# Last feed-forward sub-layer of a two-layer diffusion trunk: outputs by token rows, gate multiplied into the weights, three weight places; and another order in the opening

## The reference

```python
def rms_norm(x, g):
    y = xf * lax.rsqrt(jnp.mean(xf * xf, axis=-1, keepdims=True) + NORM_EPS)
    return y * g
def swiglu(h, w_in, w_out):
    g, u = jnp.split(h @ w_in, 2, axis=-1)
    return (jax.nn.silu(g) * u) @ w_out
def ffn_sublayer(x, g, shift, scale, gate, w_in, w_out):
    return x + FFN_RES * gate * swiglu(modulate(rms_norm(x, g), shift, scale), w_in, w_out)
...
        x = ffn_sublayer(x, g_norm[i, 2], mx[6], mx[7], mx[8], ffn_w_in[i, 1], ffn_w_out[i, 1])
    return rms_norm(x, g_final)
```

## Time and profile before

| | us |
|---|---|
| median of 3 runs (lowest, highest) | 1735.09 (1732.62, 1735.58) |
| the profiled execution | 1734.88 |
| its span, first to last instruction | 1733.1 |
| PE busy in the span | 1663.2 (96%) |
| DVE busy | 1131.4 (65%) |
| ACT busy | 610.4 (35%) |
| Silu of the first hidden tile of the last sub-layer | 1535.14 |
| last residual addition starts | 1721.27 |

### The profile page before, as it was taken

How to read it: one execution, slowest core, us unless ns; L and a number is a source line. 1 busy time by engine, 2 the same in 40 slices (tenths; PEclk the granted TensorE clock), 3 DMA queues, 4 the chain that set the end, 5 groups by cost and what they waited for, 6 DMA issues and landing times.

```text
span 1733.1 us, 24411 instructions
## 1 busy us (share of the span) xinstructions
PE 1663.2 (96%) x9083; PEld 1427.1 (82%) x9083; DVE 1131.4 (65%) x1934; ACT 610.4 (35%) x825; POOL 138.9 (8%) x82
## 2 busy tenths in 40 slices
PE   5999999999999899999999999999999879989996
PEld 3788888889777798888888988888888867889996
DVE  5778778778575778777877843743335865555555
ACT  3322221234666532212222432122123445353434
POOL 0000000001885100000000000000000222000000
PEclk9999999999999999999999999999999989989999
DMA  7655555541211135555555234422223211145553
GB/s 282 258 207 191 194 191 191 193 152 74 96 50 49 56 121 217 189 194 194 188 195 199 77 119 145 146 97 97 97 97 116 79 64 58 50 143 178 187 172 121
DMA packets 46005, 248.02 MB, mean 143 GB/s; under 512 B 5232, under 2 KB 6384, under 8 KB 25456
## 3 DMA queue, kind: packets, MB, share of 16 engines
q1 hardware_dynamic: 45936, 247.08, 39.7%
HBM read 246.01 MB, written 1.05 MB: 143 GB/s over the span
## 4 chain that ended last, share of the span: by engine, by line
PE 88%; DVE 8%; ACT 2%; issue 1%; DMA 1%; ACTq 0%; POOL 0%; SPq 0%; DVEq 0%
PE ps L1616 15%; PE ps L1618 15%; PE ps L1625 15%; PE ps L1442 10%; PE ps L1443 10%; PE ps L1444 10%; PE ps L1468 3%; PE ps L1754 3%; DVE w_lo L1094 1%; PE ps L1713 1%; PE ps L1652 1%; PE ps L1855 1%; PE ps L1785 1%; PE ps L1671 1%; DVE work L997 1%
## 5 line engine op out<-in xcount | busy, mean ns | idle before, releaser
L1616 PE MATMUL ps<-a_hi,w_hi 128*128 128x512 f32 (+1 forms) x1280 | 451.9, 363 | 3.1 <-ACT w_hi L631 3.1
L1618 PE MATMUL ps<-a_lo,w_hi 128*128 128x512 f32 (+1 forms) x1280 | 451.7, 363 | 0.0
L1094 DVE TENSOR_TENSOR w_lo<-raw,w_hi 128x2048 fp32r<-128x2048 f32 x144 | 329.3, 2289 | 86.7 <-ACT w_hi L631 49.1
L1442 PE MATMUL ps<-h_hi,w_lo 128*128 128x512 f32 (+1 forms) x824 | 285.6, 347 | 4.3 <-DVE w_lo L1094 2.8
L1443 PE MATMUL ps<-h_lo,w_hi 128*128 128x512 f32 (+1 forms) x824 | 283.6, 344 | 0.0
L1444 PE MATMUL ps<-h_hi,w_hi 128*128 128x512 f32 (+1 forms) x824 | 283.5, 344 | 0.0
L1616 PEld LDWEIGHTS ps<-a_hi,w_hi 128*128 128x128 f32 x1280 | 241.7, 189 | 41.4 <-issue 2.5
L1618 PEld LDWEIGHTS ps<-a_lo,w_hi 128*128 128x128 f32 x1280 | 241.9, 189 | 37.2
L1625 PE MATMUL ps<-a_hi,w_lo 128*128 128x512 f32 (+1 forms) x1280 | 269.1, 363 | 0.0
L1625 PEld LDWEIGHTS ps<-a_hi,w_lo 128*128 128x128 f32 x1280 | 220.1, 189 | 37.3
L625 ACT ACTIVATE work<-ps 128x512 f32<-128x512 f32 (+1 forms) x88 | 48.0, 545 | 487.2 <-PE ps L1625 466.6
(11 more groups left out here) (252 smaller groups left out, 1875.9 us busy)
## 6 DMA issues: line engine op xcount, KB each, us to landing
raw<-wstream SPq DMA_DIRECT2D x159, 1024.0 KB, 4.9
mring<-wmod SPq DMA_DIRECT2D x144, 512.0 KB, 3.5
xT<-tokens SPq DMA_DIRECT2D x4, 512.0 KB, 5.3
cb<-cond SPq DMA_DIRECT2D x1, 1024.0 KB, 6.5
out<-spare SPq DMA_DIRECT2D x8, 128.0 KB, 2.0
cst<-consts SPq DMA_DIRECT2D x1, 449.0 KB, 7.1
vec<-vecs SPq DMA_DIRECT2D x1, 174.0 KB, 7.0
ccol<-cond_cols SPq DMA_DIRECT2D x1, 8.0 KB, 1.6
```

The source lines that it names most:

```text
L1094: dve.tensor_tensor(w_lo[:, slot], raw[:, slot], w_hi[:, slot].bitcast(F32), ALU.subtract).then_inc(lo_ready, 1)
L1442: pe.matmul(dst, lhs_lo, rhs_hi, start=start, stop=False, skip_group_check=True)
L1616: pe.matmul(bank, hi, a_hi[:, k, 0:nt], start=k == 0, stop=False, skip_group_check=True)
L1618: pe.matmul(bank, hi, a_lo[:, k, 0:nt], start=False, stop=False, skip_group_check=True)
```

## The change

- **Last sub-layer, products.** The low part of the normalised latent tiles is written into columns 256 to 511 of `a_hi`, beside the high part. An input slab is now 16 matmuls of 512 columns (high weights by high and low activations at once, `last_in`) and 16 of 256 columns (low weights). The bank's two halves have to be added: DVE does this by a `tensor_reduce` over a pair for the gate and one for the up bank (`last_hidden`), and Silu and the product read SBUF.
- **Outputs by token rows.** The outputs are no longer grouped: hidden tiles go in 11 pairs, each with two input slabs and one output slab, in which the stationary operand is the hidden tile (128 tokens) and the moving one the slab (512 output features). Four banks (two token blocks by two feature halves) are kept over the whole sub-layer (`row_product`). They start from the residual, turned by 16 float32 products with the identity (`residual_rows`), 12 of them between the column sums and the spread of the norm, 4 behind the head.
- **The gate** is spread over partitions during the latent attention (8 float32 matmuls of 128 columns on PE, 2 copies on ACT) and multiplied into each raw output slab by DVE (`last_gated`) before its high part is made.
- **Three slab places**: `raw` 0, `raw` 1 and `spare`; the third place's parts lie in `h_hi` and `h_lo`.
- **End.** The squares are summed along rows by ACT (`accum_out`), one inverse root per token block, four stores; no partition sums and no spread.
- **Opening.** Eight buffers for squares, four additions of pairs, the column sums accumulate on PE; 12 matmuls on constants before them; other order of `first_products`; the low parts of slabs 0 and 1 and the high part of slab 1 one tile later; an inverse root of more than two columns takes two instructions a step for four.

The diff, cut to its core:

```diff
+        gate_row = gate_rows[:, 0:D]
+        gain_row, result = mring[:, 0], mring[:, 1:3]
+        raws = (raw[:, 0], raw[:, 1], spare[:])
+        high_slabs = (w_hi[:, 0], w_hi[:, 1], h_hi[:, 4:8].rearrange("p a n -> p (a n)"))
+        low_slabs = (w_lo[:, 0], w_lo[:, 1], h_lo[:, 4:8].rearrange("p a n -> p (a n)"))
...
+            sp.wait_ge(lo_ready, W_FFN3 + 1)
+            last_slab(2)
+            sp.dma_start(gain_row, gain.partition_broadcast(P).rearrange("p a n -> p (a n)")).then_inc(in_gain, 16)
+            with sp.Fori(0, (LAST_SLABS - 3) // 6) as i:
+                for j in range(6):
+                    sp.wait_ge(lo_ready, i * 6 + (W_FFN3 + j + 1))
+                    last_slab(3 + j, i * 6)
...
+                    if i in (2, 5):
+                        n = i // 3
+                        act.wait_ge(gate_spread, n + 1)
+                        act.activation(gate_row[:, n * 512:(n + 1) * 512], ps[2][:], ACT.Copy).then_inc(gate_copy, 1)
...
+            def last_high(r, i=None):
+                k0 = (lambda x: x) if i is None else (lambda x: x + i * 6)
+                if r >= 3:
+                    act.wait_ge(slab_done, k0(W_FFN3 + r - 2))
+                if r % 3 == 1 or r == LAST_SLABS - 1:
+                    n = r // 3 if r % 3 == 1 else LAST_PAIRS
+                    act.wait_ge(slab_gated, n if i is None else i * 2 + n)
+                else:
+                    n = last_loaded(r)
+                    act.wait_ge(raw_loaded[last_place(r)], n if i is None else i * 32 + n)
+                act.activation(high_slabs[last_place(r)], raws[last_place(r)], ACT.Copy).then_inc(hi_ready, 1)
+            def last_hidden(f, i=None):
+                k0 = (lambda x: x) if i is None else (lambda x: x + i * 4)
+                act.wait_ge(gate_sum, k0(f + 1))
+                act.activation(sil[:, f % 2, HIGH_PART], sil[:, f % 2, LOW_PART], ACT.Silu).then_inc(sil_ready, 1)
+                act.wait_ge(pair_free, k0(f0 + f + 3))
+                act.activation(h_hi[:, f % 4, HIGH_PART], prod[:, f % 2, HIGH_PART], ACT.Copy).then_inc(hhi_ready, 1)
+            def last_step(f, r, i=None):
+                for j in range(2):
+                    last_hidden(f + j, i)
+                    if r + j + 3 < LAST_SLABS:
+                        last_high(r + j + 3, i)
+                if r + 5 < LAST_SLABS:
+                    last_high(r + 5, i)
+            last_high(2)
...
+                    if n > 2:
+                        link(dve.tensor_tensor(rt[:, c], y[:, c], y[:, c], ALU.mult))
+                        last = dve.tensor_tensor(rt[:, c], rt[:, c], hv[:, c], ALU.mult)
...
-            first_squares("ffn0", TOK)
-            for k in range(2, DT):
-                add_square("ffn0", k, sq[:, k % 2], ss[:, 0])
+            for k in range(0, DT, 2):
+                dve.wait_ge(sq_ready, k + 2)
+                dve.tensor_tensor(first_sq(k), first_sq(k), first_sq(k + 1), ALU.add).then_inc(ss_sum, 2)
...
-                if k < 2:
-                    split_lo(k, k)
+                if 1 <= k < 3:
+                    split_lo(k - 1, k - 1)
...
+            def last_low(r, i=None):
+                dve.wait_ge(hi_ready, W_FFN3 + r + 1 if i is None else i * 6 + (W_FFN3 + r + 1))
+                at = last_place(r)
+                dve.tensor_tensor(low_slabs[at], raws[at], high_slabs[at].bitcast(F32), ALU.subtract).then_inc(lo_ready, 1)
...
+                pair = raws[at].rearrange("p (a n) -> p a n", a=2)
+                dve.tensor_tensor(pair, pair, gate_row.unsqueeze(1).to_broadcast([P, 2, D]), ALU.mult) \
+                   .then_inc(slab_gated, 1)
...
+                for dst, bank, done in ((sil, 2 * slot, gate_sum), (prod, 2 * slot + 1, up_sum)):
+                    dve.tensor_reduce(dst[:, slot, LOW_PART], ps[bank][:].rearrange("p (a n) -> p n a", a=2), AX.X,
+                                      ALU.add).then_inc(done, 1)
+                dve.wait_ge(up_sum, k0(f + 1))
+                dve.wait_ge(sil_ready, k0(f0 + f + 1))
+                dve.tensor_tensor(prod[:, slot, HIGH_PART], sil[:, slot, HIGH_PART], prod[:, slot, LOW_PART],
+                                  ALU.mult).then_inc(pair_free, 1)
+                dve.wait_ge(hhi_ready, k0(f0 + f + 1))
+                dve.tensor_tensor(h_lo[:, f % 4, HIGH_PART], prod[:, slot, HIGH_PART],
+                                  h_hi[:, f % 4, HIGH_PART].bitcast(F32), ALU.subtract).then_inc(hid_ready, 1)
+            def last_step(f, r, i=None):
+                last_hidden(f, r, i)
+                if r + 3 == LAST_SLABS - 1:
+                    last_gated(r + 3, i)
+                last_low(r + 3, i)
+                last_hidden(f + 1, r + 1, i)
+                if r + 5 < LAST_SLABS:
+                    last_low(r + 4, i)
+                    last_gated(r + 5, i)
+                    last_low(r + 5, i)
+            last_low(2)
+            last_hidden(0, 0)
+            last_low(3)
+            last_hidden(1, 1)
+            last_gated(4)
+            last_low(4)
+            with dve.Fori(0, LAST_TURNS) as i:
+                for _, f, r in LAST_STEPS:
+                    last_step(f, r, i)
+            for _, f, r in END_STEPS:
+                last_step(f, r)
+            dve.wait_ge(in_gain, 16)
+            for b in range(2):
+                dve.wait_ge(row_squares, 2 * b + 1)
+                dve.tensor_tensor(result[:, b, 0:512], row_bank(b, 0)[:], gain_row[:, 0:512],
+                                  ALU.mult).then_inc(row_gained, 1)
+                dve.wait_ge(row_squares, 2 * b + 2)
+                link(dve.tensor_tensor(rt[:, 2 + b:3 + b], squares[:, 2 * b:2 * b + 1],
+                                       squares[:, 2 * b + 1:2 * b + 2], ALU.add))
+                root(rt[:, 2 + b:3 + b], b, 1.0 / D, NORM_EPS)
+                dve.wait_ge(rstd_ready, CALL["final"] + b + 1)
+                dve.scalar_tensor_tensor(out=result[:, b, 512:D], in0=row_bank(b, 1)[:], scalar=ry[:, b:b + 1],
+                                         in1=gain_row[:, 512:D], op0=ALU.mult, op1=ALU.mult).then_inc(y_ready[1], 1)
...
+                    if i in (1, 4):
+                        n = i // 3
+                        if n:
+                            pe.wait_ge(gate_copy, n)
+                        for k in range(4):
+                            m = 4 * n + k
+                            last = pe.matmul(ps[2][:, k * P:(k + 1) * P], gate[:, 5, 0, m:m + 1].to_broadcast([P, P]), ident,
+                                             start=True, stop=True)
+                        last.then_inc(gate_spread, 1)
...
+            for n in range(WARM):
+                pe.matmul(ps[7][:, 0:P], ones[:], ones[:], start=True, stop=True)
+            for k in range(0, DT, 2):
+                pe.wait_ge(ss_sum, k + 2)
+                for c in range(TOK // P):
+                    last = pe.matmul(ps[NORM_BANK][:, c:c + 1], first_sq(k)[:, c * P:(c + 1) * P], ones[:, 0:1],
+                                     start=k == 0 and c == 0, stop=k == DT - 2, skip_group_check=True)
+            last.then_inc(colsum, 1)
...
+                    first_products(1, m - 2, (0, 1))
                 turn_chunk(m)
-            first_products(0, DT - 2)
-            first_products(1, DT - 3)
-            first_products(0, DT - 1)
-            first_products(1, DT - 2)
-            first_products(1, DT - 1)
+                first_products(0, m - 1, (0, 1) if m == 1 else (0, 1, 2))
+                if m == 2:
+                    first_products(0, 0, (2,))
+            first_products(1, DT - 2, (0, 1))
+            for k in range(2):
+                first_products(1, k, (2,))
+            first_products(0, DT - 1, (0, 1, 2), True)
+            first_products(1, DT - 1, (0, 1))
+            for k in range(2, DT):
+                first_products(1, k, (2,), k == DT - 1)
...
+            def residual_rows(b, h):
+                for k in range(4):
+                    pe.matmul(row_bank(b, h)[:, k * P:(k + 1) * P], xT[:, 4 * h + k, b * P:(b + 1) * P], ident,
+                              start=k == 0, stop=False, skip_group_check=True)
+            def last_in(f, r, i=None):
+                slab = W_FFN3 + r + 1
+                at = last_place(r)
+                pe.wait_ge(hi_ready, slab if i is None else i * 6 + slab)
+                pe.wait_ge(pair_free, f0 + f + 1 if i is None else i * 4 + (f0 + f + 1))
+                for t in range(2):
+                    for k in range(DT):
+                        pe.matmul(ps[2 * (f % 2) + t][:], high_slabs[at][:, t * HALF + k * P:t * HALF + (k + 1) * P], a_hi[:, k],
+                                  start=k == 0, stop=False, skip_group_check=True)
+                pe.wait_ge(lo_ready, slab if i is None else i * 6 + slab)
+                for t in range(2):
+                    for k in range(DT):
+                        last = pe.matmul(ps[2 * (f % 2) + t][:, HIGH_PART],
```

(28 more changed lines are left out.)

193 lines of the change are left out of this document (130 added, 63 removed).

## The result

| | us |
|---|---|
| median before, 6 runs (lowest, highest) | 1735.34 (1732.62, 1736.18) |
| median after, 6 runs (lowest, highest) | 1741.95 (1740.75, 1745.46) |
| ratio after to before, 95% interval | 1.0043 (1.0030 to 1.0056) |
| the profiled execution after, and its span | 1745.46, 1743.7 |

The change makes the kernel 6.6 us slower by the medians (their quotient is 1.0038, inside the interval).

The account below looks back on a forecast made before the run. PE bounds the kernel before; after the change DVE and ACT in series bound the last sub-layer. Terms 18.4 + 2.0 - 5.4 + 1.5 - 6.0 = +10.5 on 1734.88 give 1745.4 us, range 1734 to 1754.

Parts of the forecast that it names:

- The series of DVE and ACT: Last sub-layer: DVE and ACT work in turns, without overlap, 19.2 us a pair against PE's 16.5.
- B: Rival, last sub-layer: the reduction costs by its results, 0.42 us, a pair 18.5; 1738 us; chance 0.10.
- C: Rival, last sub-layer: reducing two values that lie apart costs 1.4 us, a pair 22.0; 1775 us; chance 0.07.
- PE's waits: Last sub-layer: PE waits about 2.7 us a pair, ahead of the output slab, ten times.
- The clock term: Last output slab: PE's lower clock after a wait of over 3 us costs +2 (bounds 0 and 5).
- Head: Last sub-layer's head: residual matmuls 0.4 us late in the root's wait, clock gain up to 1; together 0.
- (a): Opening: squares no longer wait for sums, -2.8 us.
- (b): Opening: root steps go from 0.61 to about 0.35 us, three times, -0.8 us.
- (c): Opening: a low slab leaves the way of the second turn, for which PE waited 2.08 us; -1.5 us.
- (d): Opening, before the first loop: 16 matmuls instead of 12 follow the first finished slab, filling PE's wait; -0.9 us.
- Attention: Latent attention: 8 float32 matmuls, 1.8 us, on PE's stream, some falling into waits; +1.5 us (1 to 2.5).
- Rival A: Last sub-layer: ACT and DVE overlap enough that PE stays the bound, pairs 16.5 us; 1712.4 us; chance 0.15.

Follow-up runs that it names:

- experiment 1: Changed kernel with the output slab's gating one step earlier in each pair, ahead of the second input slab's low part: 1711.37 us, ratio 0.9874.
- experiment 2: Changed kernel, its order kept, without multiplying the gate into the output slabs: 1717.67 us, ratio 0.9908.
- experiment 3: Changed kernel with DVE adding the halves of the gate bank twice for each hidden tile: 1756.74 us, ratio 1.0133.
- experiment 4: Changed kernel with the output slab's gating ahead of the low slab of the pair's first input slab: 1738.60 us, ratio 1.0026.
- experiment 11: Kernel of experiment 1 with the 12 residual matmuls moved behind the last sub-layer's head: 1714.69 us, ratio 0.9891.
- experiment 6: Kernel of experiment 1 with the opening's old order of first products and of slab 0 and 1 parts: 1716.43 us, ratio 0.9899.
- experiment 8: Kernel of experiment 1 with each of the 8 matmuls that spread the gate made four times: 1719.97 us, ratio 0.9920.
- experiment 5: Kernel of experiment 1 without the 12 constant matmuls ahead of the opening's column sums: 1714.36 us, ratio 0.9886.
- experiment 12: Kernel of experiment 1 with the inverse root of four columns back to four instructions a step: 1714.76 us, ratio 0.9883.

## Why the prediction was right, point by point

Forecast 1745.4, measured 1741.95, inside the range, and slower as forecast. The mechanism is settled by experiments 1 to 4: what cost the time is the length of the series in which two engines alternate; an order in which they overlap, with the same work, takes it away. Step by step:

- **PE's prices** held; a pair is 16.5 us of PE.
- **The series of DVE and ACT**: forecast 19.2 for a pair, measured 19.13; a tile 6.33 and 6.32; the reduction 0.69 and 0.683. B and C fall with that row. Beside it the Trainium skill (VectorE: DVE Perf Modes, Rules for kernel authors) calls `tensor_reduce` the slowest operation of DVE; the reduction of 512 values took 683 ns here and the product of 512 values 688, so at this size the trace does not bear it out.
- **PE's waits**: forecast 2.7 us ten times, measured 17.2 in ten. The first is 1.6, six are 2.2 to 2.4 and three about 0.6. After four of the six longer waits PE ran 3 us or so of its stream at the lower level, and the next wait in the loop was about 0.6, since the low clock had taken up the rest. The distance from pair to pair doesn't change, which is what "stays hidden in the loop" said.
- **From the first slab's end to the last matmul**: 204.5 + 2.0 forecast, 206.25 measured. The clock term is in the last matmuls: some 13 of them at 0.43 instead of 0.227, 2.6 us. Its size came out, the wait behind it did not: I had put over 3 us of waiting ahead of the last output slab, and it was 1.8 there, after which PE kept its speed, and 0.8 ahead of the slab's second half, after which it lost it. Up to the last hidden tile's low part the stage was 1.2 us shorter than forecast.
- **Head** 0: measured -0.6, less than it differs between executions (16.0 to 17.6), and it differs with PE's clock. The reason I gave beside it (the residual matmuls may keep the clock up, which gains up to 1) is left open by experiment 11. What I did not see is that a low clock under them delays the spread, as in experiments 6 and 8, where the head is some 1.5 us longer.
- **End** -5.4: measured -5.2.
- **Opening** -6.0: measured -3.8 in the profiled execution. Of the terms, (a) 2.8 is 2.4, of which 0.8 is the constant matmuls' by experiment 5 (the prediction had them only in a bound), (b) 0.8 is 0.8, (c) and (d) 2.4 are 2.5 to 2.7; by the medians of all executions they make 5.7. The profiled one is worse, by chance as far as I can tell: its tokens came 0.66 us later than in the profile of before, its column sums and its first products were slow. "About 57" for the loop's start is 57.7 at the median.
- **Attention** +1.5: measured +0.1 net. The term failed by an omission. The spread is +1.2 there, and I had counted the new root only in the opening, though the change alters every root of four columns; the one ahead of the attention gives 0.8 back. Another 0.3, between 63 and 1387 us, I can't assign: experiment 12 shows that it isn't the root near 572.
- **Rival A** (1712.4) was wrong of this kernel and right of the next: with DVE and ACT overlapped, experiment 1 gave 1711.4, and 1713.2 when run again. That it comes so close is partly luck. From the first slab's end to the last matmul A has 173.5 and experiment 1 took 175.9, of which 1.6 is the wait ahead of the first output slab; the attention and the head came out shorter than A's terms and made up for it. The Trainium skill (TensorE: Matmul & The Clock Gate, Back-to-back issue gap) would have made A about 1719 by the formula that I took from it; these runs don't agree with that. The page calls that formula the gap of an isolated matmul, which the prediction leaves out, and gives about 131 ns for a matmul of 512 columns in a stream with its weight loads; the earlier trace rows have 227.

The forecast is 3.5 us above the median. The attention term accounts for 1.4 of it and the head for at most 0.6. For the rest I have only the spread of one profile against another: executions of the changed kernel alone reach from 1740.75 to 1745.46.

## What to carry to other kernels

When two engines hand a tile back and forth, add up the series of one round, hand-overs and waits included, and hold it against the bounding engine's round: shares of busy time (here 67% and 35%) say nothing about it. A step that needs only loaded data belongs where its engine would wait for its partner, but not before its own transfer has landed: one place too late cost 30 us here and one place too early 27. Matmuls put into a wait ahead of a step on the path are free only while they fit into it; at PE's lower level these 12 took 4.5 us instead of 2.9 and no longer did. And where a helper is rewritten, price it at every call, not only at the one that the change is about.
